# Column tiles for the v rows, new stops for every body, and filling products in four waits of the first front end

## The reference, cut to what matters

```python
def block(args):
    xt, et, gt = args
    act = jax.nn.gelu(jnp.einsum('td,thkd->thk', xt, u[et]), approximate=False)
    return jnp.einsum('thk,thkd->td', gt * act, v[et])
```

## Time and profile before

| | |
|---|---|
| median of the runs | 3504.54 us (3503.97 to 3508.67, 3 runs) |
| the profiled execution | 3502.22 us, its span 3500.1 us |
| PE busy | 2942.9 us (84%) |
| DVE busy | 2341.0 us (67%) |
| POOL busy | 2008.2 us (57%) |
| ACT busy | 814.6 us (23%) |
| DMA | 1346.12 MB, mean 385 GB/s |

### The profile page before, as it was taken

The page is one execution under the profiler, slowest core; times in us unless marked ns, Lnnn a source line. Parts: engine busy times, 40 slices in busy tenths (PEclk is TensorE's granted clock), DMA queues, the critical chain, the costliest instruction groups (busy, mean ns, idle before and its releaser), DMA issues.

```text
span 3500.1 us, 34723 instructions
## 1 busy us (share of the span) xinstructions
PE 2942.9 (84%) x10960; PEld 1660.0 (47%) x10960; DVE 2341.0 (67%) x5884; ACT 814.6 (23%) x1924; POOL 2008.2 (57%) x2085
## 2 busy tenths in 40 slices
PE   7786898888997899888987799888998789976777
PEld 6465355533554355444554445544554445522222
DVE  6229756886578765887477855786648866596554
ACT  3111421133111422133211332114221232211111
POOL 1003765666565664666555655666547655577775
PEclk9897999999999999999999999999999999998999
DMA  7787999999999999999999999999999999999998
GB/s 275 259 299 266 409 409 409 408 409 402 409 402 408 399 405 403 407 409 390 405 409 408 397 351 409 409 408 370 354 409 409 409 346 350 390 404 410 409 409 339
DMA packets 387256, 1346.12 MB, mean 385 GB/s; under 512 B 41793, under 2 KB 44865, under 8 KB 386433
## 3 DMA queue, kind: packets, MB, share of 16 engines
q0 software_dynamic: 294912, 1073.87, 78.0%
q1 hardware_dynamic: 91008, 265.83, 20.1%
q10 hardware_dynamic: 1152, 4.19, 0.3%
HBM read 1334.03 MB, written 35.39 MB: 391 GB/s over the span
## 4 chain that ended last, share of the span: by engine, by line
PE 43%; DMA 25%; DVE 14%; POOL 9%; issue 6%; ACT 3%; SPq 0%; DVEq 0%; ACTq 0%; POOLq 0%
PE ps_sum L1212 19%; DMA rows<-in_peer_u,ids_u 9%; PE ps_p L979 7%; DMA rows<-in_peer_v,ids_v 6%; DMA rows<-in_peer_v,ids_u 5%; POOL rows L802 5%; PE ps_s L1127 5%; POOL rows L792 4%; DVE rows L1986 4%; DMA w_ring<-packed 2%; PE ps_s L1065 2%; PE ps_p L1073 2%; DVE feat_b L1873 1%; PE ps_p L1047 1%; DVE feat_b L1869 1%
## 5 line engine op out<-in xcount | busy, mean ns | idle before, releaser
L1212 PE MATMUL ps_sum<-rows,diag 128*128 128x512 f32 x3584 | 1748.0, 631 | 271.9 <-DMA rows<-in_peer_v,ids_v 129.2
L1986 DVE CUSTOM_DVE_ANT_0 rows<-h_cur,rows 128x1024 f32<-128x1024 f32 x1024 | 1228.1, 1220 | 539.7 <-DMA rows<-in_peer_u,ids_u 527.0
L792 POOL DMA_INDIRECT rows<-in_peer_u,ids_u x1024 | 1005.4, 982 | 720.7 <-issue 498.8
L1212 PEld LDWEIGHTS ps_sum<-rows,diag 128*128 128x128 f32 x3584 | 684.1, 201 | 1166.4 <-issue 1047.8
L802 POOL DMA_INDIRECT rows<-in_peer_v,ids_v x512 | 493.5, 964 | 452.2 <-PE ps_sum L1212 295.6
L802 POOL DMA_INDIRECT rows<-in_peer_v,ids_u x512 | 494.4, 966 | 267.8 <-issue 127.3
L1466 ACT ACTIVATE diag<-ident,acts 128x128 f32<-128x128 f32 x896 | 327.4, 394 | 1057.4 <-PE ps_sum L1212 757.5
L979 PE MATMUL ps_p<-hT,w_ring 128*128 128x128 f32 x2944 | 367.8, 286 | 36.1 <-DMA w_ring<-packed 18.0
L979 PEld LDWEIGHTS ps_p<-hT,w_ring 128*128 128x128 f32 x2944 | 362.0, 202 | 68.6 <-issue 42.3
L1772 DVE CUSTOM_DVE_ANT_0 e<-ps_s,bias_t 128x256 f32<-128x256 f32 (+6 forms) x96 | 74.2, 773 | 177.5 <-PE ps_s L1065 70.6
L2007 DVE SCALAR_TENSOR_TENSOR x_cur<-rows,acts,x_cur 128x1024 f32<-128x1024 f32 x128 | 164.0, 1282 | 13.4 <-DMA rows<-in_peer_v,ids_v 13.4
(11 more groups left out here) (280 smaller groups left out, 2325.7 us busy)
## 6 DMA issues: line engine op xcount, KB each, us to landing
w_ring<-packed SPq DMA_DIRECT2D x343, 512.0 KB, 7.7
w_ring<-in_wstream SPq DMA_DIRECT2D x65, 512.0 KB, 5.3
packed<-in_wstream SPq DMA_DIRECT2D x49, 512.0 KB, 7.9
rows<-in_peer_u,ids_u POOLq DMA_INDIRECT x1024, 13.3
rows<-in_peer_v,ids_u POOLq DMA_INDIRECT x512, 10.7
rows<-in_peer_v,ids_v POOLq DMA_INDIRECT x512, 15.4
bias_rows<-rows SPq DMA_DIRECT2D x5, 1024.0 KB, 12.8
bias_t<-in_x SPq DMA_DIRECT2D x8, 512.0 KB, 6.2
```

The source lines that it names most:

```text
L792: pool.indirect_dma_start(u_rows[:, j % G_RING, :], None, peer_u, bass.IndirectOffsetOnAxis(ap=ids_u[:, j:j + 1], axis=0)).then_inc(u_land ...
L1212: ins = pe.matmul(ps_sum[:, c * 512:(c + 1) * 512], diag[:, n % 4, :], v_rows[:, j % G_RING, c * 512:(c + 1) * 512], start=(n == 0), stop= ...
L1986: dve.tensor_tensor_reduce(row, h_cur[:, :], row, 1.0, 0.0, ALU.mult, ALU.add, dots[:, p:p + 1]).then_inc(u_used, 1)
```

## The change

- **Column tiles.** The v rows come in pairs. The ids are dealt out anew (`by_group`): the gather of an even row j brings, for tokens 0 to 63 only, their row j on partitions 0 to 63 and their row j+1 on partitions 64 to 127; the gather of j+1 does this for tokens 64 to 127. `diag` is 128 x 64 (two identities of 64 one above the other, `ident_pair`, scaled), and the product of the even row writes partitions 0 to 63 of `ps_sum`, that of the odd row partitions 64 to 127. For each half of the columns the two stand one behind the other in PE's queue. All 128 rows go this way; `on_vector` and DVE's additions are gone. A pair starts when both its rows have landed.
- **What this needs.** Gates, dots and ids are copied in four pieces of 64 partitions where they were taken whole: `hand_first_ids`, `hand_gates` and `hand_last_ids` on DVE, and Gelu in four pieces on ACT. All v gathers read `ids_v`. The ring of `diag` has 8 places instead of 4.
- **Stops.** The three tables get values of their own for each body (a few lines of them are shown).
- **Fills.** In four places of the first front end PE makes 22, 12, 12 and 26 products of `ones` and `ident`, 128 columns each, into `h_cur` before it waits: before the second half of the memory projection, in `join`, in `cross_mix`, and in `turn_scaled` of block 1. Nobody reads them.
- `gates_c`, `iota_i`, `pos_i` and `flag` share room with other tiles.

```diff
@@ the stops
-    {"latents": (1,), "mla_up": (9,), "gates": (17, 18), "recur": (20, 26), "mla_0": (29, 30, 31), "mla_1": (31, 31, 32),
...
-     "diff_2": (45, 47, 48, 49), "diff_3": (49, 49, 51, 51), "join": (54, 56), "mix_out": (56, 56, 58, 58, 58),
...
+    {"latents": (0,), "mla_up": (4,), "gates": (19, 19), "recur": (19, 26), "mla_0": (28, 32, 32), "mla_1": (32, 32, 33),
+     "mla_2": (33, 38, 38), "mla_3": (38, 38, 38), "diff_0": (38, 38, 44, 44), "diff_1": (44, 44, 44, 45),
+     "diff_2": (45, 51, 51, 51), "diff_3": (51, 51, 55, 55), "join": (65, 65), "mix_out": (65, 65, 65, 65, 65),
...
@@ program
+        low, high = slice(0, GROUP), slice(GROUP, P)
+
+        def by_group(first, last):
+
+            for at, own in ((low, low), (low, high), (high, low), (high, high)):
+                column = slice(first + (own is high), last, 2)
+                row = slice(first + (at is high), last, 2)
+                yield at, column, own, row
...
@@ POOL, gather_v
-                if on_vector(j):
-                    wait_next(v_added)
-                else:
-                    wait_next(v_used)
-                ids = ids_u if j < FIRST else ids_v
+                wait_next(v_used)
...
@@ PE
+            def fill(n):
+                for _ in range(n):
+                    ins = pe.matmul(h_cur[:, 0:P], ones[:, :], ident[:, :], start=True, stop=True)
+                ins.then_inc(filled, 1)
...
+                pair = (last - 1, last)
+                pe.wait_ge(diag_made, bp * EXPERTS + last + 1)
+                for j in pair:
                     pe.wait_ge(v_landed[j % G_RING], bp * (16 * EXPERTS // G_RING) + 16 * (j // G_RING + 1))
...
+                for c in range(2):
+                    for j, own in zip(pair, (low, high)):
+                        ins = pe.matmul(ps_sum[own, c * 512:(c + 1) * 512], diag[:, j % DIAGS, :], v_rows[:, j % G_RING, c * 512:(c + 1) * 512],
+                                        start=(last == 1), stop=(last == EXPERTS - 1), skip_group_check=True)
+                        if c:
+                            ins.then_inc(v_used, 1)
...
@@ ACT, position
-                    act.activation(acts[:, s * STEP:(s + 1) * STEP], dots[:, s * STEP:(s + 1) * STEP], ACT.Gelu).then_inc(acts_made, 1)
+                    for at, column, own, row in by_group(s * STEP, (s + 1) * STEP):
+                        ins = act.activation(acts[at, column], dots[own, row], ACT.Gelu)
+                    ins.then_inc(acts_made, 1)
...
-                    act.wait_ge(v_used, bp * SUM_ROWS + (n + SUM_SLOTS - 3))
-                    act.activation(diag[:, n % 4, :], ident[:, :], ACT.Copy, scale=coef[:, j:j + 1]).then_inc(diag_made, 1)
+                    act.wait_ge(v_used, bp * EXPERTS + (j + G_RING - DIAGS + 1))
+                    act.activation(diag[:, j % DIAGS, :], ident_pair[:, :], ACT.Copy, scale=coef[:, j:j + 1]).then_inc(diag_made, 1)
...
@@ DVE
+                for at, column, own, row in by_group(0, FIRST):
+                    dve.tensor_copy(ids_v[at, column], ids_next[own, row])
...
-                dve.tensor_copy(g_cur[:, :], g_next[:, :]).then_inc(g_handed, 1)
+                for at, column, own, row in by_group(0, EXPERTS):
+                    ins = dve.tensor_copy(g_cur[at, column], g_next[own, row])
+                ins.then_inc(g_handed, 1)
...
-                    dve.scalar_tensor_tensor(x_cur[:, :], v_rows[:, j % G_RING, :], coef[:, j:j + 1], x_cur[:, :], ALU.mult, ALU.add)\
-                       .then_inc(v_added, 1)
...
```

## The result

The changed kernel takes **3617.4 us** (median of six runs, 3608.0 to 3622.9) against 3504.3 for the kernel before: a ratio of 1.0323, interval 1.0303 to 1.0343. It is 113 us slower; 73 us faster was forecast. The profiled execution spans 3616.6 us.

A forecast was written before the change was run, and what follows sets the result against it. Behind 350 us the DMA ceiling of 409 GB/s was taken as the bound, but for dips. 3500.1 - 63.7 (dips) - 5.0 (end) - 4.8 (fills, copies) = 3426.6, adjusted to 3431 us; own range 3415 to 3446, over cases 3412 to 3472.

The forecast's parts named there:

- The added wait: PE waits for a pair's second row, up to one position (2.6 us); counted in what stays of the dips.
- What is left of the dips: Stretches under 409 GB/s after 350 us, deepest in attention of bodies 5 to 7: 77.7 us lost, 14 stay, -63.7 us.
- The new stops: Body 7's attention spreads from positions 29 to 56 to 28 to 65, into slack; no separate term in the sum.
- Rival A: DVE and stops set what is left: 46 us of the dips stay instead of 14; 3463 us, chance 0.18.
- The fills: Added PE products in four places of the first front end: -6.0 us, -4.8 us with DVE's copies.
- place (1): Before the memory projection's second half: 22 fills take 5.1 us against 2.1 us of wait; net +1.0 us.
- Place (2): In `join`: 12 fills fit into 5.58 us of idling; 24 matmuls need 10.4 us instead of 12.13; -2.2 us.
- Place (3): In `cross_mix`: 2.8 of 5.37 us idling filled; -3.8 us, if the idling that stays doesn't lower the clock again.
- Place (4): Before block 1's projection: -1.0 us.
- B: The two tiles take turns, a pair costs 3.48 us, over the deciding 3.04; 3527 us, slower, chance 0.06.
- C: Attention's chain is as long as the dip, so only the end and the fills gain; 3495 us, chance 0.06.
- D: Nothing is left of the dips (-14 us), and end, fills and first u rows gain more; 3410 us, chance 0.08.

The follow-up runs named there:

- full_pairs: The kernel before, whole, with its rows on PE taken in pairs, PE waiting for both rows and both diagonal matrices; 3591.0 us, ratio 1.0252.
- half_columns: The kernel before with the row-sum product of the second 512 columns left out for all but a block's first and last rows; 3491.5 us, 0.9968.
- tiles_old_stops: The changed kernel with the three tables of stops of the kernel before; 3558.6 us, ratio 1.0157.
- fills_only: The kernel before with the four fills and the wait for them, nothing else; 3503.0 us, ratio 0.9995.
- low_tile: tiles_old_stops with the high tile's products left out for all pairs but a block's first and last; 3554.7 us, one run.

## Why the prediction was wrong

**The ceiling** of 409 GB/s, and that the dips are all there is to gain, held. So did **the pair's price** at full clock (1.94 us, 1.74 to 2.17 forecast; the mean of 2.38 lies over it), the free change-over between 128 and 64 columns (no gap shows at it in any timeline read), ACT's sum and, nearly, DVE's, and the last pair, 2 us behind its landing. The prediction fell by three steps that lie between a correct price and the span.

*The added wait.* The prediction named what stands behind it (the next stage's products, POOL's slots), found 6 to 7 of 8 slots in use, and counted it "in what stays of the dips". So this term stood at nothing in the sum. `full_pairs` shows 88 us, 2.5%, for the wait in the kernel before, and where before takes 3716 us it cost 3.3% without tiles and 2.2% with them. It is the largest of the terms that turned the result. A bound was there to be had: a wait of up to one position in each of 512 pairs, of which only those in the dips count.

*What is left of the dips.* PE's busy time was taken as work at a fixed speed: 102 us less 24 are 78, so under the 86 of the bytes. `half_columns` tests just that, with neither tiles nor pairs, and gives 12 us instead of the 64 forecast. The clock row lay in every window that the prediction read, at 0.95 to 0.97 in the attention, and it was taken as given. In `half_columns`, where only the row sums' work shrank, it fell from 0.94 to 0.80: score products whose work had not shrunk took 3.78 us in places where they had taken 1.98, and 2 rows of half the columns took the time of 2 whole ones. In body 7's attention PE stayed busy 98.9 us, not 78. (Where before takes 3716 us the same edit gained 64 us, so this holds for the faster condition, in which the forecast was made.)

*The new stops* were said to spread the attention into positions that had slack. They cost 59 us, mostly outside the attention, where the slices are back at 409 with the old stops. Rival A named them, with POOL's wait on DVE's dots as its sign, and that is what shows (226.5 us for 169.7); it priced them at 4 us in each of six bodies, 24 us, and the measured 59 over seven are 8 each.

The account, from ratios where before takes 3503 to 3505 us: the pair's wait +88 (`full_pairs`); the tiles, the rows from DVE, the Gelus and the fills together -34 on top of it (`tiles_old_stops` less `full_pairs`, 1.0157 - 1.0252, on two chips, and with the difference in the pairs told above); the new stops +59. Sum 113, by construction: the -34 is what is left. That tiles do gain something, once pairs are paid for, fits their work; how those -34 us fall to their parts was not measured.

*The fills* were forecast at -6.0 us and gave between nothing and -3. Place by place, in the changed kernel against the earlier trace rows: place (1) cost 1.05 us, as forecast: L951's second group starts 7.3 us behind the common product (115.31), that of the earlier trace rows 6.2 us. Place (2) gained 2.0 in the changed kernel (L1136's 24 matmuls in 10.57 us: 12.13, the rest in the transposes), as forecast, and less in `fills_only`, where they took 12.26. Place (3) was mis-sized: L1171 kept its 1.97 us and L1177 went only from 6.59 to 5.65, so 0.9 and not 3.8; it was at half clock behind the 3.04 us of idling that stayed, the condition that the prediction had put to it. Place (4) gave nothing: 1.97 us again, behind 3.25 us. (The rows of place (3) would even have given 3.9 where the prediction wrote 3.8.) In `fills_only` both came at full clock, 1.09 us, behind 2.69 and the same 3.25 us, so the idling alone does not decide, and which places gain differs from run to run.

**The rivals.** B (tiles in turns) falls by `low_tile`: 1.90 and 1.94 us. It gave 3527 and had the sign right for a wrong reason. C (the pairing does nothing for the dips) is what half of the row work did, 3491 us measured, 3495 by C, though its reason, the chain of the attention alone, is not separated from the clock. D falls, as the dips grew. No rival had the pair's wait as its mechanism, and slower had got a chance of 0.06.

## What to carry to other kernels

Where PE is busy nearly all the time at full clock, time saved on it is not time gained: read the granted clock in the stretch, and price a thinning once at full and once at half clock for all else that runs there. When work is grouped to run side by side, price the wait for the last of a group by itself, at the stretch where slots are short, before the gain; the grouping alone (`full_pairs`) is a small edit and shows it. And a table of stops that belongs to another cost of rows is a change of its own, to be undone first.

## What the hardware showed that was not expected

- The granted clock fell to its lower level without a gap in PE's timeline: in `half_columns` from 2872.6 to 2880.0 the matmuls follow one another and go from 1.98 us for four of 512 columns to 3.68, at a granted clock of 0.53. With twice the row work at the same place (3.70 us for eight) it stayed up (1.00).
- Two 64-column tiles of f32 matmuls with 512 moving columns ran at once in either order of issue: 1.94 us for both, 1.90 for one.
- Products with zero weights held the clock up too (0.935 and 0.956 mean with two behind each pair, 0.84 and 0.86 without), and the time rose all the same.
- One kernel moves 364 or 409 GB/s in the same steady part, with 6% between the times of the kernel before. Two chip numbers showed the slower condition, and one of them, 8, the faster one as well. In the slower one the pair's wait cost 3.3% and half of the row work gained 1.8%, where 0.3% was gained in the faster.
- The first front end alone, the same in `before`, `full_pairs` and `half_columns`, hands its ids at 313.1, 307.6 and 307.8 us: an effect of a few us there can't be read from one trace of each.
